# Bias rows and page decays computed as jobs between the tiles of the two input projections

## What is computed

```python
def even_layer(x, norm_g, w_in, w_out, cmp_pe, cmp_w1, cmp_w2, tab, past):
    ...
    parts = split_cols(rms_norm(x, norm_g) @ w_in, EVEN_SIZES)
...
def band_attention(q, k, v, max_dist, tab, dist_scale):
    ...
    bias = tab[t5_bucket(dist * dist_scale)].reshape(Q_BLOCK, W, G, R).transpose(0, 2, 3, 1)
    p, lse = masked_softmax(s + bias, mask[None, :, :, None, None, :])
...
def fox_attention(q, q_pos, k, v, logf):
    ...
    c = jnp.cumsum(logf.astype(F32), axis=1)
    ...
        s = jnp.einsum('bqgrd,blgd->bqgrl', qg, kf) + (c_q - c_k[:, None])
...
def odd_layer(x, norm_g, w_in, b_f, w_out, past):
    ...
    q, k, v, f, z = split_cols(rms_norm(x, norm_g) @ w_in, ODD_SIZES)
    ...
    logf = jax.nn.log_sigmoid(f.astype(F32) + b_f.astype(F32))
    ...
        lf_all = jnp.concatenate([past[1].astype(F32), logf], axis=1)
```

## Time and profile before

| what | us |
|---|---|
| median of 3 runs (3823.85 to 3831.76) | 3827.74 |
| the profiled execution's own time | 3813.61 |
| its span | 3811.8 |
| PE busy in it | 3206.7 |
| block of the bias rows, from its first DMA to the next block's first | 6.93 to 109.78 |
| even projection, first DMA to last matmul | 109.78 to 619.1 |
| odd projection, last matmul | 2713.7 |
| `gates`, first DMA to the next block's first | 2717.97 to 2811.51 |

### The profile page before, as it was taken

One profiled execution on the slowest core, in us unless ns is written; L12 is line 12 of the kernel. 1 busy time (PEld: TensorE's weight loads), 2 busy tenths in 40 slices (PEclk: granted clock), 3 DMA queues, 4 the chain that ended last, 5 costly groups with the idle time before them and its releaser, 6 DMA issues. The chain is left out here.

```text
span 3811.8 us, 67405 instructions
## 1 busy us (share of the span) xinstructions
PE 3206.7 (84%) x22697; PEld 2138.3 (56%) x22697; DVE 1456.2 (38%) x4231; ACT 1003.4 (26%) x2410; POOL 580.0 (15%) x927
## 2 busy tenths in 40 slices
PE   6899997999999888996655748899768876898869
PEld 5444446988888555553524534466545554565633
DVE  0301101444443355553224547311146654554523
ACT  0100000322322356562102321100035542333311
POOL 0000001222220000002014635000011103332200
PEclk9999998999999599996668989999779997999989
DMA  1455364544442222134337965421452208999732
GB/s 32 148 206 202 135 234 119 140 121 127 123 125 55 69 69 74 54 96 125 154 119 247 300 204 182 140 71 55 135 138 54 67 24 267 330 296 313 260 150 83
DMA packets 341880, 556.86 MB, mean 146 GB/s; under 512 B 74003, under 2 KB 225083, under 8 KB 337899
## 3 DMA queue, kind: packets, MB, share of 16 engines
q1 hardware_dynamic: 265924, 355.43, 30.2%
q0 software_dynamic: 52288, 166.16, 13.6%
q10 hardware_dynamic: 23340, 30.98, 2.3%
HBM read 490.66 MB, written 118.25 MB: 160 GB/s over the span
## 5 line engine op out<-in xcount | busy, mean ns | idle before, releaser
L965 PE MATMUL PS<-cmp_xT,cmp_w 128*128 128x255 f32 (+2 forms) x2176 | 485.9, 374 | 1.1 <-DVEq L1044 1.1
L313 PE MATMUL PS<-even_w,even_xT 128*128 128x512 f32 (+1 forms) x1152 | 476.4, 574 | 1.6 <-DMA even_w<-in_w_in_e 1.6
L965 PEld LDWEIGHTS PS<-cmp_xT,cmp_w 128*128 128x128 f32 x2176 | 392.3, 191 | 47.6 <-issue 1.2
L855 ACT ACTIVATE cmp_xT<-PS 64x512 f32<-64x512 f32 x260 | 155.0, 596 | 868.5 <-PE PS L936 867.0
L313 PEld LDWEIGHTS PS<-even_w,even_xT 128*128 128x128 f32 x1152 | 218.6, 191 | 248.5 <-issue 242.6
L855 DVE COPY cmp_xT<-PS 64x512 f32<-64x512 f32 x260 | 179.3, 689 | 292.3 <-PE PS L936 290.3
L313 PE MATMUL PS<-odd_w,odd_xT 128*128 128x368 f32 x896 | 282.9, 477 | 1.4 <-DVE odd_xT L266 1.4
L313 PEld LDWEIGHTS PS<-odd_w,odd_xT 128*128 128x128 f32 x896 | 170.4, 192 | 107.1 <-issue 4.0
L873 POOL DMA_DIRECT2D cmp_pairs<-in_cache_nsa x256 | 151.6, 599 | 391.3 <-issue 391.3
L273 DVE COPY even_o<-PS 128x512 f32<-128x512 f32 (+3 forms) x81 | 50.3, 622 | 389.5 <-PE PS L313 379.0
L1597 POOL DMA_DIRECT2D s_fox_kv<-in_cache_fox x256 | 137.6, 538 | 314.9 <-issue 281.5
(11 more groups left out here) (434 smaller groups left out, 4766.9 us busy)
## 6 DMA issues: line engine op xcount, KB each, us to landing
s_fox_kv<-in_cache_fox POOLq DMA_DIRECT2D x256, 256.0 KB, 7.4
s_fox_kv<-in_cache_fox SPq DMA_DIRECT2D x256, 256.0 KB, 8.1
cmp_pairs<-in_cache_nsa POOLq DMA_DIRECT2D x256, 128.0 KB, 2.9
cmp_pairs<-in_cache_nsa SPq DMA_DIRECT2D x256, 128.0 KB, 2.9
s_sel_kv<-in_cache_nsa POOLq DMA_DIRECT2D x256, 128.0 KB, 5.0
s_sel_kv<-in_cache_nsa SPq DMA_DIRECT2D x256, 128.0 KB, 5.0
out_dil_sample<-in_cache_dil_w SPq DMA_DIRECT2D x8, 4088.0 KB, 24.4
even_w<-in_w_in_e SPq DMA_DIRECT2D x8, 2048.0 KB, 8.1
```

Of the source, the lines that this page charges most:

```text
L313: last = nc.tensor.matmul(bank(c, t, 128)[:, 0:n], xT[:, k, t * 128:t * 128 + 128], w[:, c % WS, k, 0:n], start=(k == 0), stop=(k == KT - 1))
L855: last = nc.vector.tensor_copy(dst, x) if l else nc.scalar.activation(dst, x, ACT.Copy)
L965: last = nc.tensor.matmul(hidden_ps(x, NK)[:, g], w1[:, kv, c, :], xT[:, u % 2, kv, g, c % 8, at:at + NK], start=(c == 0), stop=(c == 15))
```

## The change

The block `make_bias_rows` is gone. Its work is now in a class `BiasRows`, cut into jobs, that `project` calls in the even projection: from chunk 1 on, after each tile, PE does one job, and DVE after its eviction one. Jobs 0 to 14 are the 15 row matmuls, one each; jobs 15 to 22 are 15 matmuls with 8 columns each. The one-hot tensor of the 120 columns is now held in two halves: POOL loads the first at the start and the second into the same place once job 18 is done, and job 19, one tile later, waits for it. Loads and stores are issued by POOL.

The page decays leave `gates` and are a class `PageDecays` with 36 jobs in the odd projection, nine for each round: one carry, then a transposing and a summing one in turn, four times. There is one PSUM bank for each of the two kinds (columns 0 and 512) and one buffer `LT`, where there were two of each. DVE's reduction of the next round stands in job 5. In `gates` the waits and the DMAs for these go, and two constants are loaded in the odd projection instead.

```diff
+class PageDecays:
...
+    def gpsimd(self, pool):
...
+        for w in range(self.NP):
+            if w >= 2:
+                pool.wait_ge(self.l_turned, 4 * (w - 1))
...
+            nc.gpsimd.indirect_dma_start(self.L[:, w % 2], None, E.cache_fox_logf[0].rearrange("n p h -> n (p h)"),
+                                         bass.IndirectOffsetOnAxis(self.table[:, w:w + 1], 0)).then_inc(self.l_in[w % 2], 16)
+            if w >= 1:
+                self.store(pool, w - 1)
...
+    def tensor(self, pe, job):
+        w, x = job // self.STEPS, job % self.STEPS
...
+        if x == 0:
+            hold(self.c_in, 32)
+            hold(self.totals, w + 1)
+            hold(self.lt_ok, 4 * w)
+            nc.tensor.matmul(E.PS[:, 0:C_HEADS], self.after2[:], self.tot[:, w % 2], start=True, stop=True).then_inc(self.carried, 1)
+        elif x % 2:
...
+            hold(self.lt_ok, 4 * w + y)
+            for h in range(4):
+                last = nc.tensor.transpose(E.PS[:, 128 * h:128 * h + 128], v[:, 4 * y + h, :], E.ident[:])
+        else:
+            hold(self.lt_ok, 4 * w + y + 1)
+            hold(self.d_ok, 4 * w + y)
+            for h in range(4):
+                last = nc.tensor.matmul(E.PS[:, 512 + 128 * h:640 + 128 * h], self.LT[:, h, :], self.after[:], start=True, stop=True)
...
+class BiasRows:
...
+    def gpsimd(self, pool):
+        pool.dma_start(self.oh[:], E.c_oh_rows).then_inc(self.oh_in, 16)
+        pool.dma_start(self.ohc[:], E.c_oh_cmp_p[:, 0:60]).then_inc(self.ohc_in, 16)
...
+        pool.wait_ge(self.cmp_mm, 4)
+        pool.dma_start(self.ohc[:], E.c_oh_cmp_p[:, 60:120]).then_inc(self.ohc_in, 16)
...
+    def tensor(self, pe, job):
+        if job < 15:
...
+            hold(self.row_ok, job - 1)
+            nc.tensor.matmul(E.PS[0:nh, at:at + b - a], E.tabx[:, h0:h0 + nh], self.oh[:, k, a:b], start=True, stop=True).then_inc(self.row_mm, 1)
+        elif job < 23:
+            m = job - 15
+            hold(self.ohc_in, 16 * (m // 4 + 1))
+            for u in range(15 * (m % 4), 15 * (m % 4) + 15):
+                last = nc.tensor.matmul(E.PS[:, at:at + 8], self.ohc[:, u, :], E.tabx[:, 0:8], start=True, stop=True)
...
-        make_bias_rows(nc, E)
-        project(nc, E, "even", x_in, E.norm_e, E.w_in_e[0], E.HE, 512, 8, 280, shift_states)
+        project(nc, E, "even", x_in, E.norm_e, E.w_in_e[0], E.HE, 512, 8, 280, shift_states, BiasRows)
...
-        project(nc, E, "odd", h1, E.norm_o, E.w_in_o[0], E.HO, 368, 7, 0)
+        project(nc, E, "odd", h1, E.norm_o, E.w_in_o[0], E.HO, 368, 7, 0, None, PageDecays)
```

More of the change, by code:

```diff
@@ L160, in shift_states, with project @@
         eng.dma_start(v[1][b, 0:T - DEC_SEQ, :], v[0][b, DEC_SEQ:T, :]).then_inc(E.states, 16)
-def project(nc, E, name, sources, gain, weights, out, width, chunks, tail, with_chunk=None):
+def project(nc, E, name, sources, gain, weights, out, width, chunks, tail, with_chunk=None, beside=None):
     KT = D_MODEL // 128
@@ L172, in project @@
     with ExitStack() as s:
-        sb = lambda n, sh: s.enter_context(nc.sbuf_tensor(f"{name}_{n}", sh, F32))
+        sb = lambda n, sh, d=F32: s.enter_context(nc.sbuf_tensor(f"{name}_{n}", sh, d))
         sem = s.enter_context(signals(nc, name))
@@ L188, in project @@
         stored = [sem(f"stored{t}") for t in range(NT)]
+        job = lambda c, t: NT * (c - 1) + t
+        if beside:
+            beside = beside(nc, E, name, sb, sem, junk)
         def bank(c, t, n):
@@ L219, in _ @@
                         with_chunk(sp, E, c)
+            if beside:
+                @block.gpsimd
+                def _(pool):
+                    pool.wait_ge(xt_done, 2)
+                    beside.gpsimd(pool)
             @block.scalar
@@ L240, in _ @@
                                 act.dma_start(out[SEQ:N_ALL, at + j * q:at + j * q + q], o[32 * j:32 * j + 32, t, 0:q]).then_inc(stored[t], 16)
+                        if beside and c:
+                            beside.scalar(act, job(c, t))
                 for t in range(NT):
@@ L284, in _ @@
                     evict(0, t)
+                if beside:
+                    beside.first(dve)
                 for c in range(1, NC):
@@ L287, in _ @@
                         evict(c, t)
+                        if beside:
+                            beside.vector(dve, job(c, t))
             @block.tensor
@@ L323, in _ @@
                                 turn(t + 1)
[L326 to L374, removed]
@@ L2048, in gates @@
         bf = sb("bf", [128, C_HEADS])
-        upto, after, seq_upto = sb("upto", [128, 128]), sb("after", [128, 128]), sb("seq_upto", [N_TOK, N_TOK])
+        upto, seq_upto = sb("upto", [128, 128]), sb("seq_upto", [N_TOK, N_TOK])
         new_mask, new_bias, c_s = sb("new_mask", [N_TOK, 4]), sb("new_bias", [N_TOK, C_HEADS, 4]), sb("c_s", [N_TOK, C_HEADS])
         neg_c = sb("neg_c", [C_HEADS, SEQ])
[L2052 to L2063, removed]
+        (cin, zeroed, absd, exp_ok, one_ok, ln_ok, lf_ok, sums, c_ok, turned, neg_ok, out) = map(sem, (
+             "cin", "zeroed", "absd", "exp_ok", "one_ok", "ln_ok", "lf_ok", "sums", "c_ok", "turned", "neg_ok", "out"))
         with nc.Block() as block:
@@ L2071, in _ @@
                 sp.dma_start(bf[:], E.b_f.to_broadcast([128, C_HEADS])).then_inc(cin, 16)
-                for t, c in ((upto, E.c_upto), (after, E.c_after), (seq_upto, E.c_seq_upto), (new_mask, E.c_new_mask), (after2, E.c_after2)):
+                for t, c in ((upto, E.c_upto), (seq_upto, E.c_seq_upto), (new_mask, E.c_new_mask)):
                     sp.dma_start(t[:], c).then_inc(cin, 16)
@@ L2095, in _ @@
                 sp.wait_ge(out, 16 * (k + 4))
[L2096 to L2101, removed]
             @block.gpsimd
@@ L2105, in _ @@
                 nc.gpsimd.memset(f[:, TILES, :], 0.0).then_inc(zeroed, 1)
[L2106 to L2113, removed]
-                    nc.gpsimd.indirect_dma_start(L[:, w % 2], None, E.cache_fox_logf[0].rearrange("n p h -> n (p h)"),
-                                                 bass.IndirectOffsetOnAxis(table[:, w:w + 1], 0)).then_inc(l_in[w % 2], 16)
             @block.scalar
@@ L2122, in _ @@
                 nc.scalar.activation(e[:], e[:], ACT.Ln).then_inc(ln_ok, 1)
[L2123 to L2131 removed]
             @block.vector
             def _(dve):
[L2135 removed]
+                dve.wait_ge(cin, 16 * 13)
                 nc.vector.tensor_tensor(f[:], f[:], bf[:].unsqueeze(1).to_broadcast([128, NTI, C_HEADS]), ALU.add)
```

195 lines of the change are left out of this document (135 added, 60 removed).

## The result

| | us |
|---|---|
| median before, 4 runs (3823.82 to 3831.76) | 3825.8 |
| median after, 4 runs (3747.19 to 3766.02) | 3764.77 |
| ratio, with its 95% interval | 0.9828 (0.9805 to 0.985) |
| span of the profiled execution, before and after | 3811.8 and 3764.5 |

The forecast was 3739.9 with a range of 3718 to 3768. The direction is right and the time lies inside the range, but 25 us above the point: it is the time that rival 1 gave, 3764. So the two spans differ by 47.3 and the medians by 61.0.

The account below looks back on a forecast made before the run. PE, busy 84% of the span, was taken as the bound, so work done while it idles can be won. Terms -102.9 + 35.8 + 8 - 53 + 24.3 = -87.8 took 3827.7 to 3739.9 us, range 3718 to 3768.

Parts of the forecast that it names:

- rival 1: Even projection: bursts of narrow matmuls let the clock fall, 3 us lost at each of eight jobs, +24, 3764; chance 0.20.
- The start: Before the even projection: its first DMA moves from 109.78 to 6.93 as the bias block goes, minus 102.9 us.
- The odd projection and `gates`: Decay jobs add 24.3 us to the full PE in the odd projection; `gates` loses 53, ends 51.5 and 56.
- The wait at job 8: Odd projection, each round: job 8 needs ACT's copy of job 7; 0.5 us for each of four, 2 in all.
- The chain up to the store of `new_bias`: In `gates`: PE, DVE and ACT steps that move only by earlier arrival of their inputs, 1 to 3 us.
- The even projection: PE is full there, so jobs count whole: 35.8 us of added matmuls, plus 8 for a wait on a load.
- the price of the narrow matmuls: Even projection: 240 records at the full-clock 0.108 each, 25.9 us; all added matmuls at half clock would be 71.6.
- the wait at job 19: Even projection, chunk 3: PE waits for the second one-hot load, slowed by sharing DMA engines with copies; 8 us, ends 0 and 48.
- copies beside the load lengthen it: Chunk 3: the load needs 7.4 us alone, some 15 if it gets half of the DMA engines, landing at +25.
- take turns between queues: At the second one-hot load: by the skill's rule it goes beside SP's copies, not behind them; no trace row showed it.
- a row job: Even projection: a job of 512 columns is like an eighth of a tile, 0.88 us, ten of them 8.8.
- Switching between the streams costs nothing that shows: Even projection: jobs between tiles add no changeover cost, since eight transposes between two tiles took 0.87 us from start to start.

Follow-up runs that it names:

- experiment 1: Changed kernel with the 120 narrow matmuls cut into 24 jobs of 5 instead of 8 of 15: 3754.07 us, ratio to before 0.9806.
- experiment 5: Changed kernel with 24 jobs of 5 narrow matmuls and the second half of the one-hot tensor loaded in four quarters: 3744.22 us, ratio 0.9782.
- experiment 8: Changed kernel with 12 jobs of 10 narrow matmuls instead of 8 of 15: 3760.34 us, one execution.
- experiment 2: Changed kernel with only 1 of each 15 narrow matmuls, the other 112 left out; jobs, waits, loads and stores kept: 3733.61 us, ratio 0.9732.

## Why the prediction was right in direction and 25 us off

**The start**, -102.9: measured -102.7.

**The odd projection and `gates`**, +24.3 and -53: measured +22.1 and -53.8. The jobs run at full clock and at the lengths of rows 11. The wait at job 8 was given 0.5 each; the two gaps around the short tile, 2488.38 against 2487.84 + 0.44 and 2489.97 against 2488.38 + 1.41, are 0.1 and 0.2. The chain up to the store of `new_bias` takes 35.1 (2718.37 to 2753.50) where it took 38.1, so it is 2.9 shorter, of the 1 to 3 forecast; that the gathers' leaving did it is argued, not tested.

**The even projection**, +43.8: measured +72.0. This is the step that failed, in two terms: the price of the narrow matmuls and the wait at job 19.

The first is "At full clock the nearest row is the compression's ... I take that: 240 x 0.108 = 25.9", with the tiles behind unchanged. The eight bursts took 36.2, 10 more, and the tiles behind them 20.5 more than 6.89 each. That is 31, and 28 of it is the clock's, since at full clock the bursts would have lasted 3.44 each and the tiles behind them 7.06; rival 1 had 3 a burst, 24. The mechanism of rival 1 is shown by experiment 1, which differs from the changed kernel only in how the same 120 matmuls are cut (and with it in when the load goes out), and whose tiles are back at 7.13 wherever PE did not wait; experiment 5 shows it in two executions. I had given it a chance of 0.20, mostly because transposes between tiles did not slow the tiles. Those took 0.87 us, and experiment 1 bears out that 1.21 us of narrow matmuls leave the clock up; no row spoke for 3.4 us. Rows 12, thin matmuls at 0.50 with PE busy throughout, were the nearer rows, and they spoke for the rival.

The second term is the wait at job 19, 8. It was 1.2, since the cold tiles and slow bursts gave the load more time. The forecast also left out job 17: it stands between the short tile that ends chunk 2 and the first tile of chunk 3 (224.94 to 231.44, 6.50 long, and 3.4 at full clock). So the load was issued at +20.7 from the chunk's weights and not at +10.2, and job 19 was due at +30.1 and not at +17.2. The load landed at +31.0, where the forecast had +25. That copies beside the load lengthen it is right: it took 8.7 in experiment 8, where they had landed, 10.3 here, where the largest of them landed only at 251.8, 14.4 in another execution, and 20.7 in experiment 2, which has a wait of 14.2.

The Trainium skill, "DMA: Bandwidth & Descriptors", section "Queues, rings and completion order", has each DMA engine take turns between queues. Experiment 1 agrees in so far as its load did not come behind SP's transfers: issued 1.4 us after the chunk's weights, it landed 1.5 before them, and 7.3 before a copy of about its size that was issued 0.2 after it. The lines of the DMA issues there:

```profile
even_w<-in_w_in_e SPq DMA_DIRECT2D x1, 2048.0 KB, 14.9
out_dil_sample<-in_cache_dil_w SPq DMA_DIRECT2D x1, 1016.0 KB, 19.1
even_ohc<-const_oh_cmp_p POOLq DMA_DIRECT2D x1, 990.0 KB, 12.0
```

In the changed kernel the load landed 4.3 after the last of the copies, which tells nothing of turns.

The rest, some 4 us, is small change: a row job is 0.96 and not 0.88, and a tile with a job behind it 7.06 (86.16 to 93.22) and not 6.89 (55.13 for eight tiles in a row). "Switching between the streams costs nothing that shows" was wrong by 0.17 a job in the even projection; in the odd one it holds, with 4.95 beside a job and 4.97 without.

So 31 + 4 - 7 = 28 us in the even projection and -3 elsewhere. That makes the sum -62.4 against the forecast -87.8. Rival 1's number, 3764, was met with a larger clock term and a smaller wait, so that it fits to 1 us is luck. The time fell inside the range only because the range reached beyond the forecast's own 3753, which is itself 4 short of the terms it lists: with +-4 for the runs of before they come to 3757.

The Trainium skill, "TensorE: Matmul & The Clock Gate", Part 1, ties the 2.4 GHz to how busy PE has been, and the section "HAM oscillation — how this bites in real kernels" ties its loss to gaps in which PE is idle. The trace of this case does not agree in full: from 205.06 to 255.12 us of the changed kernel the profile has PE busy without a gap, and the clock fell. Where PE did idle, for 5.56 in experiment 1 and 14.22 in experiment 2, it fell as the page says.

What stays open is what in a burst makes the clock fall, few columns, 33 rows or the weight loads, and why bursts of 10, and in one execution those of 15, did it at some places and not at others.

## What to carry to other kernels

Small matmuls moved into a dense stream cost their own time and can cost the clock of the stream: look in the trace for a stretch of such matmuls alone, and if a record takes there about twice what it takes between tiles (0.214 against 0.115 here, though the old block's column of the granted clock reads 1.00), cut them into short jobs. Here jobs of 5 (1.2 us) kept the clock and jobs of 10 (2.3 us) kept it at some places; each further job between the even tiles also cost 0.17 us. A load that may start only when its buffer is used up needs more distance than one tile; cut the buffer so that each part is refilled many tiles ahead. When a stage's length follows the moment at which the clock rises in it, compare two kernels stage by stage, since here one such stage was 13.6 us longer in one execution than in another with nothing changed.

## What was not expected of the hardware

The granted clock was 0.74 over 100 us in which PE was busy for 98.79. The even prompt attention runs its first 80 to 100 us at 0.50 granted clock with PE busy for most of them, and two executions of one program differ there by 13.6 us (506.5 and 520.1). The second load of 1.01 MB landed after 8.7 to 20.7 us in the eight executions that have it in one piece.
